# Moving the first memory logits into the recurrence of a hybrid decoder trunk

## Chip, core and metric

The kernel runs on one core of one Trainium2 chip. The metric is the device time of one execution in microseconds.

## What is computed

Two layers work on x, 512 tokens by 1024. Each layer has a half-step of SwiGLU, a mixer, and a second half-step of SwiGLU. The mixer projects the normed x into three groups of heads: group A, sparse attention over the best 128 keys (6 heads); group B, a gated delta rule (6 heads, a recurrence over 64-token chunks); group C, attention into 256 memory tokens (4 heads). Their outputs, side by side, go through one output matrix.

```
x += 1/2 * SwiGLU_1(rmsnorm(x))
h  = rmsnorm(x); P = h @ W_in
  A: sparse attention, 6 heads x 64, top 128 of the indexer's scores, relative bias
  B: gated DeltaNet, 6 heads x 64, conv, chunked delta rule, gated RMSNorm
  C: cross-attention into 256 memory tokens, 4 heads x 64
x += concat(A, B, C) @ W_out
x += 1/2 * SwiGLU_2(rmsnorm(x))
```

## The kernel before

x stands transposed in SBUF as `xT` (128 x 8 x 512). To keep float32 accuracy, every large product is three matmuls: a value is split into a rounded high part and the rest, and `three` (lines 985 to 991) adds high by high, high by low and low by high. Activations are in `XH` and `XL`, weights in `wh` and `wl`, two buffers each, filled from `raw`. A unit of weights is 128 x 2048; SP loads it, ACT rounds it to `wh` (`split_hi`, line 1528, step "hi"), DVE subtracts to `wl` (`split_lo`, line 1908, and `split_lo_rows`, line 1900, step "lo"). Units of the mixer are numbered 0 to 19; units 14 and 15 are the value weights of group A, 16 to 19 the output matrix. Of units 16 and 17 GpSimd rounds the first half (`round_weights`, line 956) and ACT the second; all the others are rounded by ACT.

The mixer is one list of steps, `MIX_ORDER`, that `_order` writes; every engine goes through the same list and does its own part of each step. So the place of a step in the list sets its place in all five queues. The steps that matter here:

- "mm" (`group`) multiplies a slice of the contraction of one projection group. The last four groups are the values of group A for the four token blocks; they are dealt out in chunks of three 128x384 matmuls between the steps of the recurrence by `pull`. Groups alternate between PSUM banks 0 and 1; the last one had bank 2. "ev" copies a finished group out (ACT, line 1593, for the values).
- "r1", "r2", "oc", "sum", "out" are the recurrence of group B over four blocks of two chunks: PE products, DVE's U (line 2120) and state (line 2133), ACT's copies of the output, the norm. "gsplit" makes XH (ACT, line 1761) and XL (DVE, line 2147) of one third of its result.
- "sel" is one of 48 rounds of the top-128 search on DVE (line 1996 a MAX8, line 1998 a replacement).
- "att" s is a slot of a software pipeline over 40 head-and-block jobs in 13 batches (batches 0 to 3 are the memory heads; the others are group A). In slot s PE transposes the exponentials of batch s-2 (line 1414), spreads the reciprocals of batch s-3 (line 1425), computes the logits of batch s (line 1445) and multiplies the values of batch s-3 (line 1460). DVE takes the maxima of batch s (line 2159 for memory, 2172 for group A), then subtracts XL of batch s-4 where a group of heads ends (line 2184), then the reciprocals of batch s-1. ACT does the exponentials of batch s-1 (line 1774), XH of batch s-4 (1784), and copies `pT` (1792) and `oA` (1800). GpSimd multiplies `oN` of batch s-4 (924), spreads `rwide` of s-2 (933), adds mask and bias `comb` for s+2 (949).
- "rd" (`out_round`) is three 128x512 matmuls of the output matrix: for one input row block of 128 and one column block of 128. It accumulates in a PSUM bank. Rounds whose inputs come early (three of eight row blocks, FIRST_ROUNDS, then two more, SECOND_ROUNDS) are dealt out over the slots by `_early`, and "ex" adds their sum to xT on DVE (line 2220). The rest is `TAIL`, a full stream of matmuls.
- "ready" makes PE wait for all normed heads and for a group copied by ACT, before the first logits.

```
elif kind == "ready":
    pe.wait_ge(S["nq_done"], len(NORMS))
    wait_copied(N_GROUPS - 3)
```

## Time and profile before

| | us |
|---|---|
| median of 3 runs (2107.96 to 2109.15) | 2108.13 |
| the profiled execution | 2108.51 |
| its span, first to last instruction | 2106.7 |
| PE busy in it | 2079.3 |
| DVE, ACT, GpSimd busy | 1028.6, 775.2, 380.8 |

The profile is of one execution. Its engines are PE (matmuls), PEld (weight loads of PE), DVE, ACT, POOL (GpSimd) and SP, which issues transfers. A row of a timeline gives start, duration, engine, source line, operation, what it writes and reads, shapes, a count where equal ones follow each other, and in brackets the idle time before it and what ended it. The granted clock of TensorE is a share of its full speed. The two layers' mixers lie at about 400 to 700 us and 1440 to 1750 us of the span.

### The profile page before, as it was taken

Reading aid. Unit: us, or ns where it says so; the run is one execution under the profiler, and the core shown is the slowest. Engines: PE = TensorE matmul, PEld = TensorE weight load, DVE = VectorE, ACT = ScalarE, POOL = GpSimd, SP = SyncE. Lnnn points to the kernel's source line nnn. Section 1 sums busy time; section 2 is a strip of 40 time slices with the busy share of each in tenths; the row PEclk is TensorE's granted clock in tenths of the full one; section 3 lists DMA queues with packets and bytes.
Section 4 is the critical chain, followed back from the end, with each engine's and each line's share of the span. In section 5 each row is a group of like instructions: output and inputs, shape, how many; then the busy total and the mean of one; then the engine's idle time right before and its main releaser. Section 6 shows DMA issues by size and latency. Waiting matters only on the chain.

```text
span 2106.7 us, 31665 instructions
## 1 busy us (share of the span) xinstructions
PE 2079.3 (99%) x13097; PEld 1679.7 (80%) x13097; DVE 1028.6 (49%) x1391; ACT 775.2 (37%) x1058; POOL 380.8 (18%) x343
## 2 busy tenths in 40 slices
PE   9999999999999999999999999999999999999999
PEld 7888888877777888888888888887777778888887
DVE  5433333688765633333333343336887655334322
ACT  5222222475556422222232222224755554222211
POOL 1110011105025501101111110121051345111000
PEclk9999999999999999999999999999999999999999
DMA  5222222322120222222222222223212112222232
GB/s 195 87 97 100 95 90 95 123 82 78 43 91 21 100 100 100 100 90 95 95 100 100 100 91 93 101 90 127 80 63 88 45 44 98 100 100 87 94 104 75
DMA packets 30645, 192.40 MB, mean 91 GB/s; under 512 B 3216, under 2 KB 5392, under 8 KB 11984
## 3 DMA queue, kind: packets, MB, share of 16 engines
q1 hardware_dynamic: 30160, 189.80, 26.0%
q8 instruction: 77, 1.26, 0.2%
q10 hardware_dynamic: 384, 1.14, 0.1%
q14 instruction: 24, 0.20, 0.0%
HBM read 188.70 MB, written 2.10 MB: 91 GB/s over the span
## 4 chain that ended last, share of the span: by engine, by line
PE 86%; DVE 8%; ACT 4%; issue 1%; POOL 0%; DMA 0%; SPq 0%; DVEq 0%; ACTq 0%; POOLq 0%
PE psum L989 27%; PE psum L991 26%; PE psum L990 26%; DVE wl L1900 1%; PE psum L1460 1%; PE psum L1445 1%; PE psum L1414 1%; ACT wh L1528 1%; PE psum L1305 1%; PE psum L1302 1%; DVE acc L1983 1%; DVE wrk L1998 1%; DVE XL L1915 1%; DVE m L1996 1%; DVE gkT L2012 0%
## 5 line engine op out<-in xcount | busy, mean ns | idle before, releaser
L989 PE MATMUL psum<-XH,wh 128*128 128x512 f32 x1904 | 754.8, 396 | 12.5 <-DVE wl L1900 5.4
L991 PE MATMUL psum<-XH,wl 128*128 128x512 f32 x1904 | 741.9, 390 | 0.0
L990 PE MATMUL psum<-XL,wh 128*128 128x512 f32 x1904 | 741.6, 390 | 0.0
L989 PEld LDWEIGHTS psum<-XH,wh 128*128 128x128 f32 x1904 | 357.2, 188 | 109.3 <-issue 23.6
L991 PEld LDWEIGHTS psum<-XH,wl 128*128 128x128 f32 x1904 | 357.4, 188 | 75.4
L990 PEld LDWEIGHTS psum<-XL,wh 128*128 128x128 f32 x1904 | 357.6, 188 | 71.1 <-issue 1.0
L1908 DVE TENSOR_TENSOR wl<-raw,wh 128x2048 fp32r<-128x2048 f32 x88 | 201.8, 2293 | 159.4 <-ACT wh L1533 159.4
L1528 ACT ACTIVATE wh<-raw 128x2048 fp32r<-128x2048 f32 (+1 forms) x88 | 161.7, 1837 | 306.3 <-PE psum L991 306.3
L989 PE MATMUL psum<-HH,wh 128*128 128x512 f32 x704 | 273.9, 389 | 0.0
L990 PE MATMUL psum<-HL,wh 128*128 128x512 f32 x704 | 273.9, 389 | 0.0
L991 PE MATMUL psum<-HH,wl 128*128 128x512 f32 x704 | 273.9, 389 | 0.0
L835 POOL TENSOR_TENSOR sg<-sg,rF 128x512 f32<-128x512 f32 x88 | 113.7, 1294 | 783.3 <-ACT sg L1558 783.3
L1886 DVE TENSOR_TENSOR wl<-raw,wh 128x2048 fp32r<-128x2048 f32 x52 | 122.1, 2348 | 251.4 <-ACT wh L1528 251.3
L1564 ACT ACTIVATE HH<-hf 128x512 f32 (+1 forms) x88 | 55.6, 632 | 329.5 <-DVE hf L1937 329.5
L1533 ACT ACTIVATE wh<-raw 128x2048 fp32r<-128x2048 f32 x88 | 167.4, 1902 | 13.1 <-PE psum L991 13.1
L1558 ACT ACTIVATE sg<-sg 128x512 f32<-128x512 f32 x88 | 55.2, 632 | 291.8 <-DVE sg L1929 291.8
L1929 DVE TENSOR_TENSOR sg<-psum,rF 128x512 f32<-128x512 f32 x88 | 60.2, 688 | 192.4 <-PE psum L991 171.1
L991 PEld LDWEIGHTS psum<-HH,wl 128*128 128x128 f32 x704 | 132.1, 188 | 27.5
L990 PEld LDWEIGHTS psum<-HL,wh 128*128 128x128 f32 x704 | 132.1, 188 | 27.4
L989 PEld LDWEIGHTS psum<-HH,wh 128*128 128x128 f32 x704 | 132.1, 188 | 27.4
L1937 DVE TENSOR_TENSOR hf<-sg,psum 128x512 f32<-128x512 f32 x88 | 60.5, 688 | 134.2 <-PE psum L991 125.8
L757 POOL TENSOR_TENSOR sg<-xT 128x512 f32<-128x512 f32 x40 | 47.8, 1197 | 359.8 <-DVE xT L1952 333.4
(255 smaller groups left out, 1944.8 us busy)
## 6 DMA issues: line engine op xcount, KB each, us to landing
raw<-weights SPq DMA_DIRECT2D x143, 1024.0 KB, 4.8
raw<-weights SPq DMA_DIRECT2D x32, 896.0 KB, 4.4
xT<-xt SPq DMA_DIRECT2D x4, 512.0 KB, 6.4
memT<-memt SPq DMA_DIRECT2D x2, 1024.0 KB, 5.0
out<-xT SPq DMA_DIRECT2D x8, 256.0 KB, 5.8
stripsA<-strip_table SPq DMA_DIRECT2D x2, 768.0 KB, 6.7
raw<-weights SPq DMA_DIRECT2D x2, 512.0 KB, 6.6
stripsB<-strip_table SPq DMA_DIRECT2D x2, 512.0 KB, 7.2
```

The costliest lines, as they stand in the source:

```text
L835: pool.tensor_tensor(sg[fs][:, :], sg[fs][:, :], rF[:, :], ALU.mult).then_inc(S["gr_done"], 1)
L989: pe.matmul(out_ap, a_hi, b_hi, start=first, stop=False)
L990: pe.matmul(out_ap, a_hi, b_lo, start=False, stop=False)
L991: return pe.matmul(out_ap, a_lo, b_hi, start=False, stop=last)
L1528: ins = act.activation(wh[u % 2][:, k0:k1, :], raw[u % 2][:, k0:k1, :], ACT.Copy)
L1533: act.activation(wh[j][:, :, :], raw[j][:, :, :], ACT.Copy).then_inc(S["w_hi"], 1)
L1558: act.activation(sg[fs][:, :], sg[fs][:, :], ACT.Silu).then_inc(S["gs_done"], 1)
L1564: act.activation(HH[:, 2 * i + fs, :], hf[fs][:, :], ACT.Copy).then_inc(S["hh_done"], 1)
L1886: dve.tensor_tensor(wl[u % 2][:, :, :], raw[u % 2][:, :, :], wh[u % 2][:, :, :].bitcast(F32), ALU.subtract).then_inc(S["w_lo"], 1)
L1908: dve.tensor_tensor(wl[j][:, :, :], raw[j][:, :, :], wh[j][:, :, :].bitcast(F32), ALU.subtract).then_inc(S["w_lo"], 1)
L1929: dve.tensor_tensor(sg[fs][:, :], bank[fs][:, :], rF[:, :], ALU.mult).then_inc(S["g_free"], 1)
L1937: dve.tensor_tensor(hf[fs][:, :], sg[fs][:, :], bank[2 + fs][:, :], ALU.mult).then_inc(S["u_free"], 1)
```

## The change

Logits, maxima and exponentials of batch 0 are issued inside the recurrence, behind r1 of the last block. For this the exponentials become a step of their own ("exp"), the logits always use banks 0 and 2, the transposed weights use 5 and 4 (batch 0) or 5 and 1, the last value group uses bank 1, and the order of the early banks changes. GpSimd rounds both halves of units 16 and 17; unit 16 waits for the fifth slice of the last value group (`vh_done`) instead of the whole group. Rounds, selections and the halves of unit 18 are dealt to other slots. "ready" waits for one group more.

```diff
-EARLY_BANKS = (4, 6, 7)
+EARLY_BANKS = (6, 7, 4)
...
-    late = range(7, N_SLOTS)
-    spread(FIRST_ROUNDS, 1, range(2, 7), 0)
-    spread(SECOND_ROUNDS, 1, [*late, late[-1]], 1)
-    for slot, part, k0 in ((7, "hi", 0), (8, "lo", 0), (9, "hi", KD // 2), (11, "lo", KD // 2)):
+    first = [2] * 4 + [3] * 5 + [4] * 4 + [5] * 4 + [6] * 4 + [7] * 3
+    second = [8] * 3 + [9] + [s for s in range(10, N_SLOTS - 2) for _ in range(2)] + [N_SLOTS - 2, N_SLOTS - 1]
+    spread(FIRST_ROUNDS, 1, first, 0)
+    spread(SECOND_ROUNDS, 1, second, 1)
+    for slot, part, k0 in ((8, "hi", 0), (9, "lo", 0), (10, "hi", KD // 2), (12, "lo", KD // 2)):
         per_slot[slot].insert(0, (part, 18, k0, k0 + KD // 2))
...
-    return ((5, 0), (6, 7), (0, 1))[min(i, 2)][e]
+    return 2 if e else 0
...
-def weights_bank(e):
+def weights_bank(i, e):
 
-    return 2 if e else 5
+    return (1 if i else 4) if e else 5
...
-            pull(1.66)
+            pull(1.70)
...
     for step in RECURRENCE:
         order.append(step)
+        if step == ("r1", NB - 1, 0):
+            put(("att", 0), ("exp", 0))
+            continue
...
-    for slot, p in ((i, s) for i in range(N_SLOTS) for s in PAIR_SLOTS[i]):
...
+    pull(0.6)
+    put(("sum", NB - 1))
+    pull(1.0)
+    for slot in range(1, N_SLOTS):
+        if slot >= 3:
+            put(("exp", slot - 1))
+        put(("att", slot))
+        if slot == 1:
+            put(("out", NB - 1), ("exp", 1))
+            order.append(("mm", N_GROUPS - 1, fill[0][2], KD))
+            put(("gsplit", 0), ("ev", N_GROUPS - 1))
+            for v in (16, 17):
+                put(("hi", v, 0, KD // 2), ("hi", v, KD // 2, KD))
+            put(("lo", 16, 0, KD // 2), ("lo", 16, KD // 2, KD))
+        elif slot == 2:
+            put(("gsplit", 1), ("lo", 17, 0, KD // 2), ("gsplit", 2))
+        elif slot == 3:
             put(("lo", 17, KD // 2, KD))
-        if p == PAIR_SLOTS[slot][-1]:
-            put(*EARLY.get(slot, ()))
-            if slot < 8:
-                sel(1)
+        put(*EARLY.get(slot, ()))
+        sel((0, 0, 0, 2, 2, 2, 2, 1)[slot] if slot < 8 else 0)
...
-                        pool.wait_ge(S["pj_done"], LAST_OF_UNIT[U_MIX + v - 2] + 1)
+                        if v == 16:
+                            pool.wait_ge(S["vh_done"], of("vh_done", 1))
+                        else:
+                            pool.wait_ge(S["pj_done"], LAST_OF_UNIT[U_MIX + v - 2] + 1)
...
-                        elif step[0] == "hi" and step[1] in (16, 17) and step[2] == 0:
+                        elif step[0] == "hi" and step[1] in (16, 17):
                             round_weights(*step[1:])
...
-                        dst, kind = bank[2 if gi == N_GROUPS - 1 else gi % 2], g["kind"]
+                        dst, kind = bank[1 if gi == N_GROUPS - 1 else gi % 2], g["kind"]
...
                         elif kind == "ready":
                             pe.wait_ge(S["nq_done"], len(NORMS))
-                            wait_copied(N_GROUPS - 3)
+                            wait_copied(N_GROUPS - 2)
```

Three places in the queues follow. Lines of the changed kernel are 2 to 6 higher than those of before. The first place is PE's queue at the end of the recurrence, before the change. L1376 is the last output product, L989 to L991 a chunk of a value group, L1445 the logits, L1387 the sum of squares.

```order
L1376 MATMUL psum<-AT,U 64x64 x4
L989 MATMUL psum<-wh,XH 128x384 [waits w_lo]
L990 MATMUL psum<-wl,XH 128x384
L991 MATMUL psum<-wh,XL 128x384
L989 MATMUL psum<-wh,XH 128x384 [waits ev_act_0,nq_r_0,w_lo]
L990 MATMUL psum<-wl,XH 128x384
L991 MATMUL psum<-wh,XL 128x384
L1445 MATMUL psum<-mkT,mqT 128x256 [waits ev_act_0,nq_done_0]
L1445 MATMUL psum<-mkT,mqT 128x256 x3
L989 MATMUL psum<-wh,XH 128x384 [waits w_lo]
```

And the same place after it:

```order
L1380 MATMUL psum<-AT,U 64x64 x4
L989 MATMUL psum<-wh,XH 128x384 [waits w_lo]
L990 MATMUL psum<-wl,XH 128x384
L991 MATMUL psum<-wh,XL 128x384
L989 MATMUL psum<-wh,XH 128x384 [waits w_lo,ev_act_0,nq_done_0]
L990 MATMUL psum<-wl,XH 128x384
L991 MATMUL psum<-wh,XL 128x384
```

The logits are gone from here, and the chunk behind the third value group waits for a later copy by ACT (`ev_act_0`).

The second place is DVE's queue in slots 8 and 9, before. L2172 is a masked maximum, L2184 XL of finished heads, L2192 a reciprocal, L1900 the first half of wl of unit 18, L2220 an addition into xT.

```order
L2192 RECIPROCAL rrec<-rsum 128x2 [waits jb_done,je_done_0]
L1900 TENSOR_TENSOR wl<-raw,wh 128x1024 [waits hf_hi]
L2172 ISA at,mxs<-psum,comb 128x384 [waits cb_done,jl_done_0,jtr_done_0]
L2172 ISA mxs 128x1
L2172 ISA at,mxs<-psum,comb 128x384 [waits cb_done,jl_done_0]
L2172 ISA mxs 128x1
L2184 TENSOR_TENSOR XL<-oN,XH 128x3x128 [waits o_hi_0]
L2192 RECIPROCAL rrec<-rsum 128x2 [waits jb_done,je_done_0]
L2220 TENSOR_TENSOR xT<-psum,xT 128x512 [waits ex_done,pr_done]
```

After:

```order
L2198 RECIPROCAL rrec<-rsum 128x2 [waits jb_done,je_done_0]
L2178 ISA at,mxs<-psum,comb 128x384 [waits cb_done,jl_done_0,jtr_done_0]
L2178 ISA mxs 128x1
L2178 ISA at,mxs<-psum,comb 128x384 [waits cb_done,jl_done_0]
L2178 ISA mxs 128x1
L2190 TENSOR_TENSOR XL<-oN,XH 128x3x128 [waits o_hi_0]
L2198 RECIPROCAL rrec<-rsum 128x2 [waits jb_done,je_done_0]
L1906 TENSOR_TENSOR wl<-raw,wh 128x1024 [waits hf_hi]
```

wl now stands behind the maxima, XL and the reciprocal of slot 9. The third place is PE's queue in slot 9, after the change: the round that waits for this wl (`hf_lo`) is directly behind the values of slot 9, and one round is left between two slots.

```order
L1447 MATMUL psum<-dkT,dqT 128x384
L1462 MATMUL psum<-pT,dvN 64x128 [waits jp_odd_0,jp_even_0]
L1462 MATMUL psum<-pT,dvN 64x128 x7
L989 MATMUL psum<-XH,wh 128x512 [waits o_lo_0,hf_lo]
L990 MATMUL psum<-XL,wh 128x512
L991 MATMUL psum<-XH,wl 128x512
L1418 MATMUL psum<-cst,at 128x128 [waits jp_even_0,je_done_0]
```

Before, two rounds stood there, with the same wait.

## Rows read from the trace of the kernel before

**Rows 1.** The page, busy time of the engines, us (share of span) xcount
```profile
PE 2079.3 (99%) x13097; PEld 1679.7 (80%) x13097; DVE 1028.6 (49%) x1391; ACT 775.2 (37%) x1058; POOL 380.8 (18%) x343
```
**Rows 2.** The view of waits, PE: us in total, times, longest
```profile
PE psum L989 <- DVE wl L1900: 5.4, 4, 1.8
```
**Rows 3.** Timeline of PE, first layer, end of the recurrence to slot 2
```profile
600.09 0.34 PE L989 MATMUL psum<-wh,XH 128*128 128x384 f32 x1
...
607.93 1.35 PE L1414 MATMUL psum<-cst,at 128*128 128x128 f32 x8 [0.52 <-ACT at L1774]
...
611.23 0.50 PE L989 MATMUL psum<-XH,wh 128*128 128x512 f32 x1 [0.88 <-DVE wl L1900]
...
613.17 0.49 PE L989 MATMUL psum<-XH,wh 128*128 128x512 f32 x1 [0.98 <-ACT at L1774]
...
617.35 0.50 PE L989 MATMUL psum<-XH,wh 128*128 128x512 f32 x1 [1.83 <-DVE wl L1900]
```
**Rows 4.** Timeline of PE, first layer, slot 7 to the tail
```profile
648.97 0.47 PE L989 MATMUL psum<-XH,wh 128*128 128x512 f32 x1 [1.20 <-issue]
...
656.92 0.50 PE L989 MATMUL psum<-XH,wh 128*128 128x512 f32 x1
...
659.18 0.90 PE L1414 MATMUL psum<-cst,at 128*128 128x128 f32 x6 [0.60 <-ACT pT L1792]
...
678.73 0.50 PE L989 MATMUL psum<-XH,wh 128*128 128x512 f32 x1
...
679.53 0.40 PE L989 MATMUL psum<-XH,wh 128*128 128x512 f32 x1
...
680.22 0.40 PE L989 MATMUL psum<-XH,wh 128*128 128x512 f32 x1
```
**Rows 5.** Windows: us, busy of PE, PEld, DVE, ACT, POOL, PEclk, DMA, GB/s
```profile
615.00:620.00 5.00, 3.17 (x15) 2.44 (x14) 3.66 (x7) 2.57 (x10) 2.69 (x3) 0.80 0.41 174
620.00:625.00 5.00, 5.00 (x35) 3.69 (x34) 2.80 (x5) 2.41 (x8) 1.13 (x1) 0.86 0.01 3
...
1660.00:1665.00 5.00, 3.17 (x14) 2.24 (x14) 4.93 (x11) 3.60 (x11) 2.12 (x3) 1.00 0.58 210
```
**Rows 6.** Timeline of ACT, the copy of the third value group
```profile
601.26 0.58 ACT L1593 ACTIVATE dvN<-psum,rcol 128x384 f32<-128x384 f32 x1
```
**Rows 7.** Timeline of DVE, first layer, slots 1 to 16
```profile
612.83 0.68 DVE L2147 TENSOR_TENSOR XL<-gzT,XH 128x512 fp32r<-128x512 f32 x1
613.43 0.69 DVE L1996 MAX8 m<-wrk 128x8 f32<-128x512 f32 x1
...
614.82 1.28 DVE L2159 TENSOR_REDUCE mxs<-psum 128x2 f32<-128x512 f32 x2
...
616.10 1.19 DVE L1900 TENSOR_TENSOR wl<-raw,wh 128x1024 fp32r<-128x1024 f32 x1
...
653.70 1.21 DVE L1900 TENSOR_TENSOR wl<-raw,wh 128x1024 fp32r<-128x1024 f32 x1
656.10 0.56 DVE L2172 CUSTOM_DVE_ANT_0 at<-psum,comb 128x384 f32<-128x384 f32 x1 [1.19 <-issue]
...
658.69 1.30 DVE L2184 TENSOR_TENSOR XL<-oN,XH 128x384 fp32r<-128x384 f32 x1 [1.48 <-ACT XH L1784]
...
680.39 0.56 DVE L2184 TENSOR_TENSOR XL<-oN,XH 128x384 fp32r<-128x384 f32 x1 [1.99 <-ACT XH L1784]
```
**Rows 8.** GpSimd's casts of the weights: count: ns min/median/max, first and last start
```profile
L956 POOL CAST wh<-raw x4: 1037/1040/1042, 606.4 to 1654.0; 128x1024 fp32r<-128x1024 f32 x4
```
**Rows 9.** Timeline of GpSimd, first layer
```profile
609.07 0.40 POOL L933 COPY rwide<-rrec 128x256 f32<-128x256 f32 x1 [0.63 <-DVE rrec L2192]
...
616.25 1.31 POOL L933 COPY rwide<-rrec 128x256 f32<-128x256 f32 x1 [6.78 <-DVE rrec L2192]
...
653.86 3.41 POOL L949 TENSOR_TENSOR comb<-stripsA,acc 128x512 f32<-128x512 f32 x2 [1.92 <-DVE mxs L2172]
...
658.30 1.27 POOL L949 TENSOR_TENSOR comb<-stripsA,acc 128x512 f32<-128x512 f32 x1
```

More of the change, by code:

```diff
@@ L404, in _order @@
             pull(0.92)
-    assert all(name == "v" and b == 3 for name, b, _, _ in fill) and not later
+    assert fill and all(name == "v" and b == 3 for name, b, _, _ in fill) and not later
     put("ready")
-    for slot, p in ((i, s) for i in range(N_SLOTS) for s in PAIR_SLOTS[i]):
-        if p == PAIR_SLOTS[slot][0]:
-            order.append(("att", slot))
-        if p == 0:
-            pull(0.6)
-            put(("sum", NB - 1))
-            pull(1.0)
-            put(("out", NB - 1))
-        if p == 1:
-            pull(9.0)
-            put(("hi", 16, 0, KD // 2))
-        if p == 2:
-            put(("gsplit", 0), ("hi", 16, KD // 2, KD), ("lo", 16, 0, KD // 2), ("gsplit", 1))
-        if p == 3:
-            put(("hi", 17, 0, KD // 2), ("lo", 16, KD // 2, KD), ("gsplit", 2))
-        if p == 4:
-            put(("lo", 17, 0, KD // 2), ("hi", 17, KD // 2, KD))
-        if p == 7:
+    pull(0.6)
[15 more added lines that the diff above has]
+        elif slot == 3:
             put(("lo", 17, KD // 2, KD))
-        if p == PAIR_SLOTS[slot][-1]:
-            put(*EARLY.get(slot, ()))
-            if slot < 8:
-                sel(1)
+        put(*EARLY.get(slot, ()))
+        sel((0, 0, 0, 2, 2, 2, 2, 1)[slot] if slot < 8 else 0)
     put(*TAIL)
@@ L1097, in group @@
                                 mm = three(dst[:, 0:WA], (XH[:, k, tok], XL[:, k, tok]), (v_hi, v_lo), first, last)
+                                if gi == N_GROUPS - 1 and k == V_SPLIT - 1:
+                                    mm.then_inc(S["vh_done"], 1)
                             elif kind == "M":
@@ L1587, in evac @@
                         act.wait_ge(S["pj_done"], gi + 1)
-                        name, b, src = g["name"], g["b"], bank[2 if gi == N_GROUPS - 1 else gi % 2]
+                        name, b, src = g["name"], g["b"], bank[1 if gi == N_GROUPS - 1 else gi % 2]
                         if name == "mv":
@@ L1761, in gdn, with exponentials @@
                             act.activation(XH[:, 3 + c, :], gzT[:, c, :], ACT.Copy).then_inc(S["gh_done"], 1)
-                    def attention(slot):
-                        i = slot - 1
+                    def exponentials(i):
                         if 0 <= i < N_BATCHES:
@@ L1776, in attention @@
                                                ).then_inc(S["je_done"], 1)
+                    def attention(slot):
                         i = slot - 4
@@ L1791, in attention @@
                                     act.wait_ge(S["jv_done"], JOBS_BEFORE[i - 1])
-                                act.activation(pT[i % 2][:, e, 0:bank_width(i)], bank[weights_bank(e)][:, 0:bank_width(i)], ACT.Copy
+                                act.activation(pT[i % 2][:, e, 0:bank_width(i)], bank[weights_bank(i, e)][:, 0:bank_width(i)], ACT.Copy
                                                ).then_inc(S["jp_odd" if e else "jp_even"], 1)
@@ L1821, in layer @@
                             attention(*at_)
+                        elif kind == "exp":
+                            exponentials(*at_)
                         elif kind == "hi":
```

56 lines of the change are left out of this document (26 added, 30 removed).

## The prediction

> **What bounds the kernel now.** I read the busy shares first. PE is busy 99% of the span [rows 1], but a busy PE is not PE at its peak; what a reordering can win is PE's idle time, and the view of waits lists it. It holds 27 us in all, and the largest entry is PE waiting for DVE's low halves of the weights [rows 2]. Then I read PE's timeline where the recurrence hands over to attention. Up to 607.4 us the queue is full. Then come four holes of 0.52, 0.88, 0.98 and 1.83 us, 4.2 us in all; the second and the fourth end when DVE has written the wl of units 16 and 17 that an output round reads [rows 3]. Further on there are two more: 1.20 us at 648.97, ahead of the first of the SECOND_ROUNDS, and 0.60 us at 659.18 [rows 4]. The second layer repeats both pictures some 1045 us later. So each layer has 6.0 us of holes here, and nothing else in the kernel is touched by the change.
>
> The clock takes a further share. In the slices 615 to 620 and 620 to 625 the granted clock is 0.80 and 0.86, right after the four holes; in the second layer, behind the same holes, it is 1.00 [rows 5]. One fall costs 5 x 0.20 + 5 x 0.14 = 1.7 us. At the low level of 1.2 GHz a stretch takes twice as long as at 2.4 GHz.
>
> **The change, part by part, per layer.** No instruction is added or dropped but the place of each is new; DMA issues keep their order and sizes. So the sum goes over holes: those that vanish and those that appear.
>
> (a) First logits inside the recurrence. Eight matmuls (4 products) move ahead of r2(3,0), in place of one value chunk; DVE does two maxima of 0.64 us in place of one selection, and ACT, idle there, does four exponentials. PE's work is the same, so it is worth nothing by itself. What it had covered is the point: before, PE ran a chunk of the last value group, the logits and another chunk from 600.09 on, while ACT copied the third value group out of its bank; that copy ran from 601.26 to 601.84 [rows 3, 6]. Now the last value group is in bank 1, which that third group leaves, and "ready" waits for the copy. PE has only "ready" and chunks of the last group in its queue. Price: 601.84 - 600.09 = 1.75, with the restart **+1.8 us**. ACT is idle where the exponentials now go, so they don't push this copy back. Behind the waiting PE stand the sum of squares, the second logits and all that follows.
>
> (b) The four holes go: **-4.2 us**. The transposes of batch 0 find their exponentials done, and the second logits run beside the value chunks.
>
> (c) Two holes come in their place. PE's first output round waits for XL and wl of unit 16, which now stand on DVE behind the second maxima and "out". From ACT's copy on, DVE needs 0.68 + 1.2 us; PE has 8 transposes and 4 logits products, about 1 us less: 0.85 us. Then PE has three rounds of 0.69 us (680.22 - 679.53, [rows 4]) while DVE does wl, two maxima and XL, 1.2 + 1.28 + 0.68 = 3.2 us [rows 7]: 1.1 us. Lower bound 1.9 us. The upper one comes from GpSimd. It now does four casts of 1.04 us [rows 8] back to back, just while DVE does these. Before, two casts met only operations on PSUM. Where GpSimd and DVE meet on SBUF, one waits: rwide took 1.31 us instead of 0.40 when wl, 1.19 us, had started 0.15 us before it [rows 7, 9]; XL took 1.30 us instead of 0.56 when comb had started 0.39 us before it [rows 7, 9]. In both pairs the later one ended about one own duration after the earlier one. A cast ahead of XL and wl, and one more ahead of the second XL, add 2.3 us: upper bound 4.2 us. I take **+3.2 us**, nearer to the upper bound because these rows are the same pairing. The Trainium skill ("SBUF — State Buffer", who interferes with whom) says that a DVE instruction with two SBUF inputs and a GpSimd instruction that reads SBUF exclude each other for whole instructions; by that rule the term would be the full 4.2, and if they merely shared bandwidth it would be near 1.9.
>
> (d) The SECOND_ROUNDS start behind attention slot 8, no longer 7: **-1.2 us** (the hole at 648.97 goes, as DVE has written that XL a slot earlier).
>
> (e) The half "lo 18" moves from slot 8 to slot 9, onto DVE behind the whole of slot 9's attention work, and the round that needs it, (2,3,0), stands on PE directly behind its own part of slot 9. Before, wl was written from 653.70 for 1.21 us and PE used it at 656.92 [rows 4, 7]. Now DVE must first do the two masked maxima from 656.10, then XL, which waited for ACT's half and for GpSimd and ended at 659.99, then the reciprocal and then wl: not before 661.2, where PE is ready at 656.92. That is 4.3 us in the times of before. GpSimd loses the wait for the moved wl (two combs took 3.41 us where two take 2 x 1.27, [rows 9]), so the chain can come 0.9 us earlier; XL without a block saves 0.74 more, and with slot 8 longer by two rounds another 0.2. On the other side comb can block wl for 1.27 us. Bounds 4.3 - 0.9 - 0.7 - 0.2 = 2.5 and 4.3 - 0.9 + 1.3 = 4.7 us; I take **+3.8 us**. The hole of 0.60 us at 659.18 vanishes behind it: **-0.6 us**.
>
> (f) Rounds are dealt two to a slot, so only two (1.4 us) are left behind the last values of slot 15, where there were four. The tail's first round needs the last XL, which ended at 680.95, and PE's last values ended at 678.73 [rows 4, 7]: 2.2 - 1.4, with a semaphore, **+0.9 us**.
>
> (g) Two selections in each of slots 3 to 6: a selection is a MAX8 of 0.69 us and a replacement of the same size [rows 7], so 2.8 us of DVE where a slot of PE is some 5.7 us (an attention part of 2.9, four rounds of 0.69). With maxima, XL and additions the DVE queue is nearly full and runs about 1 us late, but a logits product waits only for the maxima of the slot before. Nothing; if that cover is gone, it is 0.5 us a slot.
>
> Sum: 1.8 - 4.2 + 3.2 - 1.2 + 3.8 - 0.6 + 0.9 = +3.7 us a layer, +7.4 in both. The clock fell once in four holes; now there are four places with holes of 2 us and more, one of nearly 4 us of silence in each layer. I count two falls for one: +1.7. The profiled execution took 2108.5 us, the median is 0.4 lower: 2108.5 + 9.1 - 0.4 = **2117.2 us**.
>
> **The rivals.**
> *The engines don't block each other.* Then (c) is 1.9 and (e) 2.5, +1.1 a layer, and the clock falls once as now: 2110.3 us. For it: half of the rows that look blocked could be late issues. Against: two different pairs show the same sum.
> *The wait for wl of unit 18 is covered, and the change gains.* It decides at one point: DVE has to be through with wl 2.8 us after PE enters slot 9. If ACT's half and GpSimd's product come earlier, since slot 8 is now two rounds longer, (e) is 0; with (c) at 1.9 the sum is -1.4 a layer, and with less silence the clock keeps its upper level, -1.7: 2108.5 - 2.8 - 1.7 - 0.4 = 2103.6 us. Against it: DVE's two masked maxima (0.56 each from 656.10) end at 657.2 and wl takes 1.21 more, so 1.5 us would remain even if XL cost nothing.
> *More falls of the clock, all blocks in full.* (c) 4.2, (e) 4.7: +5.6 a layer, and three falls more than now, 5.1 us: 2124.4 us.
> *The change doesn't do what it says.* GpSimd rounds alone only units 16 and 17; unit 18 stays with ACT. The order shows the first logits inside the recurrence, so nothing is left to this one.
>
> **How the numbers follow.** Forecast 0.50 (2112.5 to 2121), no blocking 0.27, covered wait 0.13, more falls 0.10. About 0.2%, 4.2 us, is what a measurement of this kernel can tell from no change, so slower means above 2112.3 and faster below 2103.9. The forecast and the last rival are slower, 0.60; the second case is the same, 0.27; the third is faster, 0.13. The range reaches from inside the no-blocking case and part of the covered one, 2105.5, to 2122.5.
>
> **What would show it.** Right: a hole of 1.8 us on PE in front of the last value group, released by ACT's copy; holes of 2 and about 1.5 us before the first and fourth output round, with casts on GpSimd beside lengthened XL or wl; no hole before slot 8; a hole of 3 to 5 us ahead of round (2,3,0), released by DVE's wl; 0.9 us ahead of the tail. Wrong: if PE runs through slot 9 without a hole, (e) falls and with it the sign; if casts overlap wl at 1.04 and 1.2 us, the blocking falls.

## The result, and the profile after

| | before | after |
|---|---|---|
| median (lowest to highest of 10 runs each) | 2108.24 (2106.59 to 2109.39) | 2114.00 (2112.41 to 2115.83) |
| the profiled execution | 2108.51 | 2115.3 |
| its span | 2106.7 | 2113.4 |

All times are microseconds. The ratio is 1.0028, 95% interval 1.002 to 1.0037. The change makes the kernel slower by 5.8 us. The busy times of the engines hardly moved [rows 1]:

```profile
PE 2081.5 (98%) x13097; PEld 1683.0 (80%) x13097; DVE 1033.5 (49%) x1391; ACT 773.5 (37%) x1054; POOL 389.1 (18%) x347
```

The view of waits has the answer to [rows 2]. The columns are what PE waited for, us in total, times, longest one.

```profile
PE psum L989 <- DVE wl L1906: 10.7, 4, 2.9
PE psum L989 <- ACT dvN L1595: 3.5, 2, 1.8
...
PE psum L989 <- DVE XL L2153: 1.9, 2, 1.0
...
PE psum L989 <- issue: 1.3, 2, 0.6
```

PE's wait for DVE's low halves doubled, from 5.4 to 10.7 us, in as many places. The copy `dvN` by ACT and the XL of the recurrence are new in the list; "issue" stood for the hole ahead of slot 8 before (2.4 us in all) and stands for the one ahead of the tail now. PE's timeline shows where these waits are. These are all the places from 590 us to the end of the first layer's mixer with an idle time over 0.3 us; they answer to [rows 3, 4].

```profile
602.10 0.41 PE L989 MATMUL psum<-wh,XH 128*128 128x384 f32 x1 [1.75 <-ACT dvN L1595]
...
612.87 0.50 PE L989 MATMUL psum<-XH,wh 128*128 128x512 f32 x1 [2.48 <-DVE wl L1906]
...
616.15 0.47 PE L989 MATMUL psum<-XH,wh 128*128 128x512 f32 x1 [0.95 <-DVE XL L2153]
...
656.44 0.79 PE L989 MATMUL psum<-XH,wh 128*128 128x512 f32 x1 [2.88 <-DVE wl L1906]
...
683.62 0.47 PE L989 MATMUL psum<-XH,wh 128*128 128x512 f32 x1 [0.65 <-issue]
```

Five holes, 8.7 us, stand where six stood with 6.0 us. The second layer has the same five, 8.7 us again. These holes are 5.4 us more than before, and the span grew by 6.7. The difference is not the clock alone; it is a larger loss and a gain, taken apart below. The windows answer to [rows 5]: us, busy of PE, PEld, DVE, ACT, POOL, granted clock, DMA share, GB/s.

```profile
655.00:660.00 5.00, 3.56 (x12) 2.83 (x14) 1.39 (x1) 2.34 (x7) 3.44 (x4) 0.56 0.02 3
660.00:665.00 5.00, 5.00 (x29) 2.96 (x27) 3.04 (x8) 2.09 (x5) 1.89 (x2) 0.76 0.00 0
1650.00:1655.00 5.00, 3.55 (x11) 2.98 (x12) 0.31 (x1) 1.68 (x5) 1.00 (x1) 0.73 0.00 0
1655.00:1660.00 5.00, 5.00 (x32) 4.30 (x31) 2.21 (x4) 2.58 (x10) 2.12 (x2) 0.93 0.00 0
1705.00:1710.00 5.00, 2.60 (x9) 2.21 (x10) 2.35 (x3) 2.58 (x8) 4.40 (x4) 0.69 0.00 0
```

The clock falls behind three holes: the 2.88 in both layers and the 1.75 of the second layer. Before, it fell once.

What a fall costs can be read where the same work runs with and without one. The first two rows are the changed kernel, from the last chunk ahead of the hole of 1.75 us to the transposes behind it, in either layer. The other two are the kernel before, from the round behind the hole of 1.83 us to the next rounds.

```profile
599.55:608.28 8.73, 6.98 (x41) 5.77 (x38) 2.72 (x5) 4.54 (x14) 2.33 (x3) 1.00 0.00 0
1648.90:1659.21 10.31, 8.56 (x41) 6.96 (x38) 2.71 (x5) 4.54 (x13) 2.33 (x3) 0.83 0.00 0
```

```profile
617.35:623.05 5.70, 5.70 (x38) 4.45 (x38) 2.16 (x5) 1.31 (x4) 1.59 (x3) 0.70 0.01 3
1663.98:1668.07 4.09, 4.09 (x38) 3.19 (x38) 2.17 (x5) 1.21 (x4) 1.60 (x3) 1.00 0.00 0
```

Each of these falls costs 1.6 us. The two falls behind the holes of 2.88 us cost 2.8 and 1.4 us: from the values ahead of the hole to the next rounds PE takes 10.29 us (652.47 to 662.76) and 8.88 us (1703.42 to 1712.30), where a kernel shown further down takes 7.50 us for the same work and the same hole at clock 1.00. So the clock costs 5.8 us in this execution and 1.6 in the one of before. Now the whole stretch in which the kernels differ, from the idle time of 0.68 us ahead of L1339 (now L1343) to the end of the mixer, in both layers, before and after:

```profile
583.66:717.39 133.73, 127.56 (x941) 98.17 (x941) 85.33 (x169) 69.43 (x161) 64.26 (x68) 0.99 0.18 63
1630.29:1762.37 132.08, 125.91 (x941) 96.92 (x941) 85.26 (x169) 69.31 (x161) 64.25 (x68) 1.00 0.18 64
```

```profile
583.41:719.56 136.15, 127.30 (x938) 98.35 (x938) 87.75 (x169) 68.02 (x159) 68.65 (x70) 0.97 0.18 62
1632.77:1769.09 136.32, 127.50 (x937) 98.90 (x938) 87.70 (x169) 68.01 (x159) 68.64 (x70) 0.97 0.18 62
```

It holds the whole growth of the span. Without its falls a mixer takes 132.1 us before and 133.4 now: 1.3 us more a layer, though its holes are 2.7 us more. The other work and the smaller idle times have become 1.4 us shorter a layer. So the 6.7 us are 5.4 of holes and 4.1 of the clock, less 2.8 of other work and smaller idle times.

Now the queue of DVE around the first output round, which answers to [rows 7]:

```profile
609.39 1.44 DVE L2153 TENSOR_TENSOR XL<-gzT,XH 128x512 fp32r<-128x512 f32 x1 [0.99 <-ACT XH L1763]
610.76 3.38 DVE L1906 TENSOR_TENSOR wl<-raw,wh 128x1024 fp32r<-128x1024 f32 x2
```

and GpSimd in the same stretch, which answers to [rows 9]:

```profile
606.95 4.79 POOL L956 CAST wh<-raw 128x1024 fp32r<-128x1024 f32 x4 [4.39 <-PE psum L991]
```

Beside the four casts XL takes 1.44 us, where 0.68 stood before, two wl take 3.38, where one took 1.19, and the casts take 4.79, where one took 1.04. Both sides are stretched. And this is DVE around slot 9:

```profile
652.67 0.56 DVE L2178 CUSTOM_DVE_ANT_0 at<-psum,comb 128x384 f32<-128x384 f32 x1 [3.25 <-issue]
...
653.63 0.55 DVE L2190 TENSOR_TENSOR XL<-oN,XH 128x384 fp32r<-128x384 f32 x1
...
654.17 2.21 DVE L1906 TENSOR_TENSOR wl<-raw,wh 128x1024 fp32r<-128x1024 f32 x1
```

DVE idles 3.25 us ahead of slot 9's maxima. ACT's half of unit 18 is there since 650.2, in the middle of that idle time, and yet its wl starts at 654.17, because it stands behind slot 9 in the queue:

```profile
649.12 1.06 ACT L1530 ACTIVATE wh<-raw 128x1024 fp32r<-128x1024 f32 x1
```

### The profile page after: what moved, and what is told of

It is laid out like the page before. It is cut to its first block and busy times, and to the rows that moved or that the text cites. A ratio compares the mean times of both kernels' runs of the same rounds, so it can differ in the third digit from the quotient of the medians.

```text
span 2113.4 us, 31663 instructions
## 1 busy us (share of the span) xinstructions
PE 2081.5 (98%) x13097; PEld 1683.0 (80%) x13097; DVE 1033.5 (49%) x1391; ACT 773.5 (37%) x1054; POOL 389.1 (18%) x347
## 5 line engine op out<-in xcount | busy, mean ns | idle before, releaser
L989 PE MATMUL psum<-XH,wh 128*128 128x512 f32 x1904 | 755.4, 397 | 16.6 <-DVE wl L1906 10.7
L991 PE MATMUL psum<-XH,wl 128*128 128x512 f32 x1904 | 742.2, 390 | 0.0
L989 PEld LDWEIGHTS psum<-XH,wh 128*128 128x128 f32 x1904 | 357.4, 188 | 113.7 <-issue 25.6
L991 PEld LDWEIGHTS psum<-XH,wl 128*128 128x128 f32 x1904 | 357.7, 188 | 75.3
L989 PE MATMUL psum<-HH,wh 128*128 128x512 f32 x704 | 273.9, 389 | 0.0
L991 PE MATMUL psum<-HH,wl 128*128 128x512 f32 x704 | 273.9, 389 | 0.0
L1530 ACT ACTIVATE wh<-raw 128x2048 fp32r<-128x2048 f32 (+1 forms) x84 | 157.4, 1873 | 306.7 <-PE psum L991 306.5
L991 PEld LDWEIGHTS psum<-HH,wl 128*128 128x128 f32 x704 | 132.1, 188 | 27.6
L989 PEld LDWEIGHTS psum<-HH,wh 128*128 128x128 f32 x704 | 132.1, 188 | 27.4
L990 PEld LDWEIGHTS psum<-HL,wh 128*128 128x128 f32 x704 | 132.1, 188 | 27.3
```

The costliest lines, as they stand in the source:

```text
L989: pe.matmul(out_ap, a_hi, b_hi, start=first, stop=False)
L990: pe.matmul(out_ap, a_hi, b_lo, start=False, stop=False)
L991: return pe.matmul(out_ap, a_lo, b_hi, start=False, stop=last)
L1530: ins = act.activation(wh[u % 2][:, k0:k1, :], raw[u % 2][:, k0:k1, :], ACT.Copy)
```

## The experiments

Unless the text says otherwise each kernel is the changed one with one edit, and is compared with its median of 2114.0. "Before" ran beside each group: its medians were 2107.78, 2108.15 and 2108.36. Counted against before of its own group, each difference moves by up to 0.5 us.

### wl of unit 18 back ahead of slot 9

```diff
-    for slot, part, k0 in ((8, "hi", 0), (9, "lo", 0), ...
-        per_slot[slot].insert(0, (part, 18, k0, k0 + KD // 2))
+    for slot, part, k0 in ((8, "hi", 0), (8, "lo", 0), ...
+        per_slot[slot].insert(len(per_slot[slot]) if (slot, part) == (8, "lo") else 0, (part, 18, k0, k0 + KD // 2))
```

> The changed kernel, with one step moved back: the first half of wl of unit 18 stands at the end of slot 8, ahead of slot 9's maxima, instead of behind slot 9's reciprocal. Main theory (the wait was made by the place on DVE alone): in the changed kernel DVE was idle from 649.4 to 652.7 us and ACT's half was there at 650.2, so wl is written by 651.5 to 652.5. The hole of 2.88 us falls to about 0.6, what XL of slot 9 (ended 654.18) leaves behind PE's values (ended 653.56). Two layers: -4.5 us of holes. The falls of the clock that followed these holes (slices 655 to 665 at 0.56 and 0.76, 1705 to 1715 at 0.69 and 0.97) should be gone too, up to -3.4 and -1.7 us, part of it already counted as hole. Time 2106 to 2109.5, against 2114.0. Rival (GpSimd's masked sums are on the path: wl beside them blocks them, and slot 9's maxima come later by as much): a hole of 2 us and more stays on PE in slot 9 or at the transposes after it, and the time is 2112 to 2115.

Measured: 2106.43 (2104.84 to 2108.47), 7.6 us less than the changed kernel; against before 0.9995 (0.9986 to 1.0004), no difference. The hole of 2.88 is gone, and 0.45 us has come at the transposes behind it. These are DVE's wl and PE's next hole:

```profile
649.89 1.67 DVE L1906 TENSOR_TENSOR wl<-raw,wh 128x1024 fp32r<-128x1024 f32 x1 [0.79 <-ACT wh L1530]
652.35 0.56 DVE L2178 CUSTOM_DVE_ANT_0 at<-psum,comb 128x384 f32<-128x384 f32 x1 [0.80 <-PE psum L1447]
```

```profile
654.60 0.90 PE L1418 MATMUL psum<-cst,at 128*128 128x128 f32 x6 [0.45 <-ACT pT L1796]
```

GpSimd's two masked sums were stretched by this wl, from 2.52 to 3.51 us, as the rival had it, but slot 9's maxima came no later for it: the last thing they waited for was PE. Holes explain 2 x (2.88 - 0.45) = 4.9 us. In this profile the clock is 1.00 in every slice of both mixers, and 2.7 us more are gone than the holes hold; that these are the falls is tried by the pair further down. One step's place on one engine is worth more than the whole difference between the two kernels.

### The same move alone, in the kernel before

```diff
-    for slot, part, k0 in ((7, "hi", 0), (8, "lo", 0), (9, "hi", KD // 2), (11, "lo", KD // 2)):
+    for slot, part, k0 in ((8, "hi", 0), (9, "lo", 0), (10, "hi", KD // 2), (12, "lo", KD // 2)):
```

> The kernel before, with nothing changed but the slots of the four halves of unit 18: 8, 9, 10, 12 as in the changed kernel, instead of 7, 8, 9, 11. Main theory (this one move makes the slower kernel slower): a hole of 2.5 to 4 us opens ahead of the first round of slot 9, released by DVE's wl; the hole of 0.60 us at 659.18 goes; +2 to +3.4 us a layer, 2112 to 2114.5 against 2107.8, and up to 3 us more for falls of the clock behind the new holes. Rival (the hole needs the changed kernel's other moves, such as three rounds in slot 8): the hole is under 1.5 us and the time 2107.5 to 2109.5.

Measured: 2118.66 (2117.73 to 2121.0), ratio 1.0053 (1.0039 to 1.0067), 10.5 us slower than before.

```profile
660.07 0.53 PE L989 MATMUL psum<-XH,wh 128*128 128x512 f32 x1 [4.36 <-DVE wl L1900]
```

```profile
656.51 1.29 DVE L2184 TENSOR_TENSOR XL<-oN,XH 128x384 fp32r<-128x384 f32 x1 [0.66 <-ACT XH L1784]
...
657.80 2.21 DVE L1900 TENSOR_TENSOR wl<-raw,wh 128x1024 fp32r<-128x1024 f32 x1
```

The theory is right and its size too small. The hole is 4.36 us, the one of 0.60 us is gone, so the holes account for 2 x 3.76 = 7.5 us; the other 3.0 us came with more falls of the clock. Its profile has four where that of before has one: behind the 4.36 us in both layers (0.66 and 0.50 in the slices from 660 and 1710), at the old holes of the second layer (0.89 and 0.77), and one near the start (0.85 and 0.81 from 5 to 15). The move harms the old kernel more than the new one. There XL waits 0.66 us for ACT's half and is stretched (1.29 against 0.55 us); in the changed kernel it does neither. These 1.4 us are nearly all of the difference between 4.36 and 2.88. Slot 8 is one round long there instead of three, which leaves GpSimd and ACT less time ahead of it; that this is the reason was not tried.

### The last value group in bank 7

```diff
-                            if gi == N_GROUPS - 1:
-                                wait_copied(gi - 1)
+                            if gi == N_GROUPS - 1:
+                                pe.wait_ge(S["s_done"], of("s_done", 2 * NB - 1))
...
-                        dst, kind = bank[1 if gi == N_GROUPS - 1 else gi % 2], g["kind"]
+                        dst, kind = bank[7 if gi == N_GROUPS - 1 else gi % 2], g["kind"]
...
+                            if (r, i) in STARTS and nth_bank == 1:
+                                wait_copied(N_GROUPS - 1)
...
-                            wait_copied(N_GROUPS - 2)
+                            wait_copied(N_GROUPS - 3)
...
-                        name, b, src = g["name"], g["b"], bank[1 if gi == N_GROUPS - 1 else gi % 2]
+                        name, b, src = g["name"], g["b"], bank[7 if gi == N_GROUPS - 1 else gi % 2]
```

> The changed kernel, with the last value group in bank 7, which the recurrence's state has left by then, instead of bank 1, so that it need not wait for ACT's copy of the third group. Main theory: the hole of 1.75 us ahead of the last group goes (a rest of about 0.3 us may stay ahead of the sum of squares, which waits for ACT's squares), and everything behind it, GpSimd's casts too (they wait for PE's fifth slice of this group), comes earlier by the same: -3.5 us of holes in both layers, and -1.7 for the fall of the clock that followed this hole in the second layer: 2108.8 to 2110.5, against 2114.0. Rival (the chain through ACT's exponentials, GpSimd and DVE is the bound there, and PE only waits earlier): the 1.75 us come back in the hole ahead of the first output round, which grows from 2.5 to about 4 us, and the time stays at 2113 to 2115.

Measured: 2111.51 (2109.93 to 2112.75), 2.5 us less. The hole of 1.75 is gone in both layers and no other one grew; the next is the same as before, only earlier:

```profile
611.23 0.50 PE L989 MATMUL psum<-XH,wh 128*128 128x512 f32 x1 [2.48 <-DVE wl L1908]
```

The rival is out. The gain is 1.0 us short of the 3.5 us of holes, and the clock, which I had expected to gain, still fell in this profile (0.97 and 0.69 in the first layer, 0.82, 0.83, 0.76 and 0.90 in the second, behind the holes of 2.48 and 2.88). Removing one cause of silence doesn't remove the falls while larger ones are left.

### Two engines round units 16 and 17 again

```diff
-            for v in (16, 17):
-                put(("hi", v, 0, KD // 2), ("hi", v, KD // 2, KD))
+            put(("hi", 16, 0, KD // 2), ("hi", 16, KD // 2, KD), ("hi", 17, 0, KD // 2))
...
-            put(("gsplit", 1), ("lo", 17, 0, KD // 2), ("gsplit", 2))
+            put(("gsplit", 1), ("lo", 17, 0, KD // 2), ("gsplit", 2), ("hi", 17, KD // 2, KD))
...
-                        elif step[0] == "hi" and step[1] in (16, 17):
+                        elif step[0] == "hi" and step[1] in (16, 17) and step[2] == 0:
                             round_weights(*step[1:])
...
-                            elif v < 16:
+                            elif v < 18:
                                 act.wait_ge(S["pj_done"], LAST_OF_UNIT[U_MIX + v - 2] + 1)
-                            if v not in (16, 17):
+                            if v not in (16, 17) or k0:
                                 split_hi(U0 + U_MIX + v, k0, k1)
```

> The changed kernel, with the second halves of units 16 and 17 rounded by ACT again (GpSimd does two casts in a row instead of four). Main theory (a cast on GpSimd and a subtraction on DVE that meet on SBUF stretch each other): the XL that took 1.44 us at 609.39 falls towards 0.66, the two wl that took 3.38 us towards 2 x 1.2, the casts from 1.2 towards 1.04 us each, and the hole ahead of the first output round from 2.48 to about 1.3 us: -2.4 us in both layers, 2111.6, less what ACT's 1.06 us ahead of pT cost. Rival (no blocking; these lengths are pipeline overlap in the records): the lengths stay, the holes stay within 0.3 us, ACT's extra work delays pT and the exponentials of batch 2, and the time is 2114 to 2116.

Measured: 2111.15 (2109.83 to 2113.51), 2.9 us less. PE's two holes, DVE and GpSimd:

```profile
611.20 0.50 PE L988 MATMUL psum<-XH,wh 128*128 128x512 f32 x1 [1.10 <-DVE wl L1905]
...
614.29 0.47 PE L988 MATMUL psum<-XH,wh 128*128 128x512 f32 x1 [0.75 <-DVE XL L2152]
```

```profile
609.11 0.70 DVE L2152 TENSOR_TENSOR XL<-gzT,XH 128x512 fp32r<-128x512 f32 x1 [0.99 <-ACT XH L1762]
609.73 2.55 DVE L1905 TENSOR_TENSOR wl<-raw,wh 128x1024 fp32r<-128x1024 f32 x2
```

```profile
606.67 1.04 POOL L955 CAST wh<-raw 128x1024 fp32r<-128x1024 f32 x1 [4.38 <-PE psum L990]
```

With two casts taken away, XL is 0.70 instead of 1.44 us, the two wl 2.55 instead of 3.38, and the casts that are left 1.04 each (the second is the same from 608.23). So the lengths in the changed kernel were mutual stretching and no artefact of the records. Holes fell by 2.48 + 0.95 - 1.10 - 0.75 = 1.6 us a layer, 3.2 in both; ACT's added work shows in the 0.3 us that are missing, if anywhere.

### One more round ahead of the tail

```diff
-    second = [8] * 3 + [9] + [s for s in range(10, N_SLOTS - 2) for _ in range(2)] + [N_SLOTS - 2, N_SLOTS - 1]
+    second = [8] * 3 + [9] + [s for s in range(10, N_SLOTS - 3) for _ in range(2)] + [N_SLOTS - 3, N_SLOTS - 2, N_SLOTS - 1, N_SLOTS - 1]
```

> The changed kernel, with one round of the second group of rounds moved from slot 14 to slot 16, so that two rounds (instead of one) stand between the last values and the tail. Main theory: the hole of 0.65 us ahead of the tail's first round goes, as 0.7 us of matmuls cover it: -1.3 us in both layers, 2112.7 against 2114.0. Rival (slot 14 needs its two rounds as cover): a hole of the same size opens in slot 15 at the transposes or values, and the time stays at 2114.0.

Measured: 2112.69 (2112.03 to 2115.06), 1.3 us less, with no hole in slots 14 to 16 or ahead of the tail. The difference is smaller than the spread of either kernel's runs, and against before of the same group it is 0.9; that the hole vanished is read from the timeline, the time only agrees.

### wl of unit 16 ahead of the first XL

```diff
-            put(("gsplit", 0), ("ev", N_GROUPS - 1))
+            put(("lo", 16, 0, KD // 2), ("gsplit", 0), ("ev", N_GROUPS - 1))
...
-            put(("lo", 16, 0, KD // 2), ("lo", 16, KD // 2, KD))
+            put(("lo", 16, KD // 2, KD))
```

> The changed kernel, with the first half of wl of unit 16 put ahead of the first XL on DVE (it stood behind it). In the changed kernel DVE idled 0.99 us, from 608.40, for ACT's XH, while GpSimd's first cast was done at about 608.1. Main theory (work order on DVE sets the first output round): wl runs in that idle time, XL behind it ends near 611.1, and the hole of 2.48 us ahead of the first output round falls to 1.0 to 1.5 us; the hole of 0.95 us before the fourth round stays or grows by up to 0.3. Sum -2 us over both layers, 2111 to 2112.5, against 2114.0. Rival (GpSimd's casts hold DVE up wherever it stands, so the moved wl only waits for the second cast): the hole stays above 2.2 us and the time at 2114.

Measured: 2115.06 (2113.25 to 2116.91), not faster than the changed kernel. Both theories missed: the first hole did fall, to 1.54 us, and the second rose from 0.95 to 1.56. DVE and GpSimd:

```profile
610.54 2.05 DVE L1906 TENSOR_TENSOR wl<-raw,wh 128x1024 fp32r<-128x1024 f32 x1
612.51 1.52 DVE L2153 TENSOR_TENSOR XL<-gzT,XH 128x512 fp32r<-128x512 f32 x1
613.95 2.06 DVE L1906 TENSOR_TENSOR wl<-raw,wh 128x1024 fp32r<-128x1024 f32 x1
```

```profile
609.16 5.78 POOL L956 CAST wh<-raw 128x1024 fp32r<-128x1024 f32 x4 [5.99 <-PE psum L991]
```

Every one of DVE's three is stretched now by 0.8 to 0.9 us, and the casts take 5.78 us instead of 4.79. While four casts run, a DVE order that starts earlier only meets more of them. In this profile the clock also fell in both layers behind the holes of 1.75 and 2.88.

### Useless matmuls in the hole of slot 9

```diff
                     for step in MIX_ORDER:
                         kind, *at_ = step
+                        if step == ("rd", 2, OUT_ORDER[0], 0):
+                            for _ in range(4):
...
+                                three(bank[early_bank(OUT_ORDER[2], True)][:, :], (wh[1][w], wl[1][w]),
+                                      (XH[:, k, :], XL[:, k, :]), False, False)
```

> The changed kernel, with useless matmuls in the hole of slot 9: ahead of round (2,3,0), four times the three products of round (1,5,1) are added into its open bank once more, 12 matmuls of 0.23 us, 2.76 us in each layer, where PE idled 2.88 us. The result is not the reference's: one input block counts five times in one column block of each mixer's output. The wait for wl stays as it is, only the silence on PE goes. Main theory (part of the loss in slot 9 is the clock, which falls behind a hole of this length): the granted clock stays 1.00 in slices 655 to 665 and 1705 to 1715, and the time falls by what the run with the early wl had more than its holes account for, 7.6 - 4.9 = 2.7 us: 2111.3, between 2110.5 and 2112.5. Rival (the falls come with the count or share of holes at large, not with this one): a fall appears elsewhere, and the time is 2113.5 to 2115.

Measured: 2112.52 (2109.94 to 2115.52), 1.5 us less, with a spread of 5.6 us. The clock was 1.00 around slot 9 in both layers, but fell in the first layer behind the holes of 2.48 and 0.95 (0.92 and 0.74 in the slices 610 to 620). Each theory has one half. Too noisy to price the clock: hence the pair below, in a kernel that is quiet elsewhere.

### The four repairs together

The edits of unit 18, bank 7, the two rounding engines and the tail.

> The changed kernel with four repairs together: wl of unit 18 at the end of slot 8, last value group in bank 7, second halves of units 16 and 17 on ACT, one more round in slot 16. Main theory (the terms add): holes per layer 1.75 to 0, 2.48 to 1.1, 0.95 to 0.75, 2.88 to 0.45, 0.65 to 0, so 8.7 to 2.3 us, -12.8 us in both, and 2.7 us for the clock: 2098.5, between 2097.5 and 2102, faster than both kernels. Rival (the repairs share one cover: with bank 7 PE arrives 1.75 us earlier at an output round that ACT's and DVE's chain releases): the hole ahead of the first output round is 2 to 2.8 us and the time is 2102 to 2105.

Measured: 2097.85 (2097.23 to 2098.19), ratio to before 0.995 (0.9937 to 0.9964), 10.3 us faster than before and 16.2 than the changed kernel. PE's holes in the first layer, all that are left over 0.3 us:

```profile
610.39 0.50 PE L988 MATMUL psum<-XH,wh 128*128 128x512 f32 x1 [1.10 <-DVE wl L1907]
...
613.48 0.47 PE L988 MATMUL psum<-XH,wh 128*128 128x512 f32 x1 [0.76 <-DVE XL L2154]
...
652.25 0.90 PE L1419 MATMUL psum<-cst,at 128*128 128x128 f32 x6 [0.45 <-ACT pT L1797]
```

The terms add: 2.3 us of holes a layer, as expected, and a clock of 1.00 in every slice of both mixers. Five runs lie within 1.0 us, where those of the changed kernel span 3.4.

### The price of the clock: the late wl, silent and filled

Both are the kernel with the four repairs without the one for unit 18; the second has the useless matmuls in the hole as well.

> The combination of four repairs (2097.85 us, clock 1.00 throughout) with the one for unit 18 taken out: wl stands behind slot 9's work again. Main theory (the wait costs its hole and a fall of the clock behind it): the hole is 2.88 us in place of 0.45, +4.9 us in both layers, and a slice or two behind each hole at 0.6 to 0.9 bring +1.5 to +3: 2104.2 to 2105.8. Rival (without the other holes ahead of it, one hole does not bring the clock down): the clock stays 1.00 and the time is 2102.7, within 0.8.

> The same kernel with the late wl, with the useless 12 matmuls of 0.23 us in its hole in both layers (one input block counts five times in one column block, so the result is not the reference's). Main theory (the fall follows the silence): the wait is as long but the clock stays 1.00, so the time is 2102.7, within 0.8, and the difference to the kernel with the silent hole is the price of the clock, 1.5 to 3 us. Rival (the clock is not set by this hole): both kernels with the late wl take the same time, within 0.8 us.

Measured: silent 2104.45 (2103.29 to 2105.66), filled 2101.86 (2101.25 to 2102.68). The two ranges don't touch. PE waits for wl as long in both, so 2.6 us, 1.3 a layer on average, are the clock. Silent against the four repairs it is 6.6 us, 4.9 of holes and 1.7 over. In the silent kernel's profile the clock fell in one layer only, behind the 2.88, so the two layers give the price of one fall. From the values ahead of the hole to the next rounds:

```profile
649.35:656.85 7.50, 4.62 (x45) 3.10 (x43) 4.33 (x8) 4.24 (x11) 5.27 (x6) 1.00 0.01 3
1692.02:1701.10 9.08, 6.20 (x45) 4.26 (x43) 4.33 (x8) 4.38 (x11) 5.26 (x6) 0.81 0.00 0
```

The same stretch takes 7.53 us in both layers when the hole is filled, with no slice of the mixers below 1.00. So a silence that no fall follows costs nothing beyond the wait, and this fall costs 1.6 us. At that price the 2.6 us between the medians are fewer than two falls in an execution. The Trainium skill ("TensorE: Matmul & The Clock Gate", part 1) says that the reduced clock is the default and activity releases it; the pair agrees, since matmuls that nobody needs were enough to keep 1.00.

### The first logits back out of the recurrence

In the kernel with the four repairs:

```diff
     for step in RECURRENCE:
         order.append(step)
-        if step == ("r1", NB - 1, 0):
-            put(("att", 0), ("exp", 0))
-            continue
...
     pull(0.6)
+    put(("att", 0), ("exp", 0))
     put(("sum", NB - 1))
```

> The combination of four repairs with the first logits, maxima and exponentials moved back out of the recurrence, behind the first chunks of the last value group. This tells what the early logits, the change's own idea, are worth. Main theory (they were worth their holes): the second batch's logits need the banks that the first batch's exponentials read, which end 1.3 (maxima) + 1.9 (exponentials) us behind the first logits, where PE has 1.5 to 2 us of other work: a hole of 1 to 2 us ahead of the second logits, +2 to +4 us in both layers: 2100 to 2102, against 2097.85. Rival (the last group's four chunks cover it): 2097.5 to 2098.5.

Measured: 2099.15 (2099.05 to 2099.8), 1.3 us slower than the four repairs, less than expected.

```profile
604.70 1.13 PE L1446 MATMUL psum<-mkT,mqT 64*128 64x256 f32 x8 [0.85 <-ACT at L1775]
```

The hole at the second logits is there, 0.85 us, and the next is 0.15 longer (1.25), but the 0.45 us in slot 9 is gone. With them the holes of a layer are 2.9 us instead of 2.3, 1.1 us in both. So the early logits, after which the change is named, are worth 1.3 us here. Most of the 4.2 us of old holes must have gone by the rest, the steps and banks that let PE run value chunks, transposes and second logits in one piece; that part wasn't tried by itself.

### DVE's order on top of the four repairs

```diff
+        if slot == 1:
+            put(("out", NB - 1))
         put(("att", slot))
         if slot == 1:
-            put(("out", NB - 1), ("exp", 1))
+            put(("exp", 1))
...
-            put(("gsplit", 0), ("ev", N_GROUPS - 1))
+            put(("lo", 16, 0, KD // 2), ("gsplit", 0), ("ev", N_GROUPS - 1))
...
-            put(("lo", 16, 0, KD // 2), ("lo", 16, KD // 2, KD))
+            put(("lo", 16, KD // 2, KD))
```

> The combination of four repairs, with DVE's order changed around the first output round: the product gzT of the last block ahead of the maxima of batch 1 (DVE idled 3.6 us there), and the first half of wl of unit 16 ahead of the first XL, in the time in which DVE waited for ACT's XH. Only two casts on GpSimd meet them. Main theory (DVE's order is what is left): the hole of 1.10 us ahead of the first output round falls to 0.5 or less, the one of 0.76 stays within 0.3: -1 to -1.5 us in both layers, 2096.4 to 2097, against 2097.85. Rival (as in the run with wl of unit 16 first: what one hole gives the next takes, since DVE's sum of work to the fourth round is the same and wl meets a cast): the time is 2097.5 to 2098.3.

Measured: 2096.57 (2096.39 to 2096.88), 1.3 us less than the four repairs, which had run on another chip; ratio to before 0.9949 (0.9936 to 0.9963). This is the fastest of all. The first hole fell from 1.10 to 0.41 us, the second rose from 0.76 to 0.93. DVE and GpSimd here:

```profile
606.95 1.23 DVE L1909 TENSOR_TENSOR wl<-raw,wh 128x1024 fp32r<-128x1024 f32 x1 [0.46 <-POOL wh L957]
608.32 1.29 DVE L2156 TENSOR_TENSOR XL<-gzT,XH 128x512 fp32r<-128x512 f32 x1
```

```profile
605.88 1.04 POOL L957 CAST wh<-raw 128x1024 fp32r<-128x1024 f32 x1 [2.80 <-PE psum L992]
607.43 1.63 POOL L957 CAST wh<-raw 128x1024 fp32r<-128x1024 f32 x1 [0.52 <-PE psum L992]
```

Here the pairs are clean enough to follow one by one. wl runs at its own length from 606.95 to 608.18. The cast that starts inside it ends at 609.06, one own duration (1.04) after 608.02. XL starts inside the cast and ends at 609.61, one own duration (0.68) after 608.93. Each later one ends as if it had done its work only when the earlier one was through, within 0.2 us.

## Why the prediction was right, and where its sizes were off

Forecast 2117.2, measured 2114.0; slower was forecast and came. The holes that it named are there and have the causes that it gave. That the total came so near is in part luck: the holes were taken 2.0 us too large, the clock too small, and a gain of 2.8 us wasn't in the sum at all. By its own steps, per layer:

| step | forecast | measured |
|---|---|---|
| (a) last value group waits for ACT's copy | +1.8 | +1.75 |
| (b) four old holes | -4.2 | -4.2 |
| (c) first and fourth output round | +3.2 (1.9 to 4.2) | +3.4 (2.48 and 0.95) |
| (d) hole ahead of the SECOND_ROUNDS | -1.2 | -1.2 |
| (e) wl of unit 18 behind slot 9 | +3.8 (2.5 to 4.7) | +2.9 |
| (e) hole at 659.18 | -0.6 | -0.6 |
| (f) tail | +0.9 | +0.65 |
| sum | +3.7 | +2.7 |

**The mechanisms hold** for the new holes, each with an edit that took it away: (a) by bank 7, (c) by the two rounding engines, (e) by the early wl and once more in the kernel before, (f) by the added round. Of (b) only the early logits were tried; (d) and the 0.60 us at 659.18 are read from the timeline. For (g), the doubled selections, I made no run; PE has no hole in slots 3 to 7, as forecast.

**(e) was mis-sized** and is most of the 1.0 us a layer by which the sum of holes was too large. From 4.3 I allowed gains of 0.9, 0.7 and 0.2 us, set a loss of 1.3 against them, and took 3.8. Put into the kernel before, the move costs 4.36, near my 4.3; in the changed kernel it costs 2.88. So the other moves are worth 1.5 us, not 0.5: XL neither waits 0.66 us for ACT's half nor is stretched (0.55 us against 1.29). The loss that I set against them, comb holding wl up, is real (wl takes 2.21 us), but it is there in both kernels and no reason to take less off.

**(c) was right in sum, not in its halves.** I had expected 2 and 1.5 us. The first is longer, because XL and wl are both stretched ahead of it, and what the first hole costs, the next is spared. The run with wl first shifted it (1.54 and 1.56, 3.1 us against 3.4). The trace decides between the two ways to cost it: 3.4 us lie above the 1.9 of no interference and below the 4.2 of full exclusion. The rule of the Trainium skill ("SBUF — State Buffer", who interferes with whom), that the two engines exclude each other for whole instructions, agrees with the two clean pairs of the last run and with those of [rows 7, 9]. The full 4.2 didn't come because not every meeting that I counted took place: XL and the two wl were lengthened by 0.76 + 1.0 us, where I had put 2.3, and the XL ahead of the fourth round met no cast (0.66 us).

**The clock** was +1.7 for both layers, as one fall more than before. In the two profiled executions it is 5.8 - 1.6 = +4.1: three falls for one. The price of a fall was right (1.7 forecast, 1.6 measured), the count was not. The medians can only be estimated. In the group of the run with the early wl, three executions of before show a clock of 1.000 and took 2106.2 to 2106.5, about 1.5 below their median. Three of the early wl itself do, and took 2104.8 to 2105.4; with the 4.9 us of hole between the two kernels that makes some 2109.9 for the changed one without falls, 4.1 below its median. By this estimate the change adds 2.6 us of clock.

**A term put at nothing.** Step (a) says that PE's work is the same, so it is worth nothing by itself, and the sum goes over holes alone. At a clock of 1.00 throughout, PE is busy 125.9 us in the second layer's stretch before and 124.7 in the same stretch of the run with the early wl (1627.57 to 1758.72), with the same matmuls. The order alone saves 1.2 us a layer; smaller idle times give the rest of the 1.4. The early logits are a part of it: the four repairs are busy 124.7 us there (1624.53 to 1751.83) and the late logits 125.1 (1624.70 to 1752.92). The rest was not taken apart. So at equal clock the change costs 1.3 us a layer and not the 2.7 of its holes.

**The rivals.** Engines that don't block each other (2110.3) is refuted by the run with two rounding engines. The covered wait (2103.6) is refuted: DVE was 2.88 us late. It was near in one respect, since the wait could be covered by moving one step. More falls and all blocks in full (2124.4) is refuted by (c) and (e); of its three falls more than before, two came.

## What to carry to other kernels

When a list of steps sets the order of every engine, a step that is moved "one slot later" lands behind all that this slot puts on its engine. Look for the idle time ahead of that work: here DVE idled 3.25 us in front of the maxima and the weights stood behind them, at a price of 7.6 us. Before you give an idle engine more SBUF work, ask which DVE instructions it meets there; halving the casts gave back 2.9 us. A silence of PE may cost more than its length (here 1.3 us on average for one of 2.88, 1.6 where the clock fell and nothing where it didn't), and the clock's share isn't to be read from one profile, nor taken as what the holes leave over: here 1.3 us were left over, and the clock was 4.1, because the new order also saved 2.8.

## What the runs showed of the hardware that was not expected

The stretching is mutual. I had looked for longer DVE instructions only; four casts on GpSimd took 4.79 and 5.78 us instead of 4 x 1.04 when DVE's subtractions ran beside them.

The place of a fall varies from kernel to kernel more than the holes do. The same hole of 2.48 us, followed by one of 0.95, had the clock at 1.00 in the changed kernel and in the run with the early wl, and was followed by a fall in the run with the useless matmuls. The early wl still has the holes of 1.75 and 2.48, and three of its eleven executions have a clock of 1.000. In the four kernels that have none of the holes of 1.75, 1.83, 2.48 and 2.88 (the four repairs, the late logits, DVE's order, the filled late wl) no slice of the mixers was below 1.00 in the profile, and the runs of each lie within 0.5 to 1.4 us, where those of the others span 2.4 to 5.6. What the falls of one execution depend on, beyond the silence ahead of them, stays open.
